# The last 32 tokens of a PEER layer leave the dense table products and are gathered instead

## The reference, cut to what matters

```
def peer(h, wq, subkeys, u_tab, v_tab):        # h: 256 x 1024; u_tab, v_tab: 16384 x 1024
    q = (h @ wq).reshape(256, 8, 2, 64)        # 8 heads, two halves
    s = einsum('thpd,hpnd->thpn', q, subkeys)  # 128 scores for each half
    sv, si = top_k(s, 16)
    cand = sv[:, :, 0, :, None] + sv[:, :, 1, None, :]      # 16 x 16
    best, pos = top_k(cand, 16)
    eidx = the expert numbers (row * 128 + column) of the 16 best
    gates = softmax(best)
    act = gelu(einsum('td,thkd->thk', h, u_tab[eidx]))
    w = gates * act
    return einsum('thk,thkd->td', w, v_tab[eidx])
```

## Time and profile before

| what | value |
|---|---|
| median of 3 runs | 1016.75 us |
| profiled execution, span of its instructions | 1014.6 us |
| what lies around the span (median less span) | about 2.15 us |
| PE busy | 998.4 us (98%) |
| DVE, ACT, POOL busy | 773.9, 506.5, 323.3 us |
| DMA | 222.78 MB, 220 GB/s over the span |

### The profile page before, as it was taken

One profiled execution on the slowest core, in us unless ns is written; L12 is line 12 of the kernel. 1 busy time (PEld: TensorE's weight loads), 2 busy tenths in 40 slices (PEclk: granted clock), 3 DMA queues, 4 the chain that ended last, 5 costly groups with the idle time before them and its releaser, 6 DMA issues.

```text
span 1014.6 us, 17813 instructions
## 1 busy us (share of the span) xinstructions
PE 998.4 (98%) x6803; PEld 920.8 (91%) x6803; DVE 773.9 (76%) x1580; ACT 506.5 (50%) x730; POOL 323.3 (32%) x206
## 2 busy tenths in 40 slices
PE   8999999999999999999999999999999999999996
PEld 8899889999999999999999999988888888888885
DVE  6979887883998798886678788766665867777666
ACT  4676556455444544445443443454554554454443
POOL 1001000112776678786778867000010000000002
PEclk9999999999999999999999999999999999999999
DMA  9989858776555687777666766677678788887761
GB/s 358 369 286 378 291 195 302 258 222 219 181 176 182 163 192 187 185 187 177 161 153 146 160 147 146 185 217 221 217 238 310 228 253 259 266 265 228 222 206 48
DMA packets 96852, 222.78 MB, mean 220 GB/s; under 512 B 27520, under 2 KB 45952, under 8 KB 96000
## 3 DMA queue, kind: packets, MB, share of 16 engines
q1 hardware_dynamic: 74336, 207.93, 63.4%
q0 software_dynamic: 22144, 13.71, 8.9%
q10 hardware_dynamic: 288, 0.01, 0.0%
HBM read 211.06 MB, written 10.55 MB: 218 GB/s over the span
## 4 chain that ended last, share of the span: by engine, by line
PE 88%; DVE 5%; DMA 2%; ACT 2%; issue 1%; POOL 1%; POOLq 0%; ACTq 0%; DVEq 0%
PE px L1148 33%; PE pw L842 16%; PE pw L843 16%; PE pw L844 16%; PE px L1124 3%; DMA raw<-in_w 2%; DVE w_lo L1204 1%; PE px L1093 1%; DVE lo L1226 1%; DVE ada L1243 0%; ACT hi L563 0%; PE px L1027 0%; ACT w_hi L563 0%; PE px L1010 0%; ACT h2f L734 0%
## 5 line engine op out<-in xcount | busy, mean ns | idle before, releaser
L563 ACT ACTIVATE w_hi<-raw 128x1024 fp32r<-128x1024 f32 x312 | 328.7, 1057 | 314.6 <-PE px L1148 151.7
L1204 DVE TENSOR_TENSOR w_lo<-raw,w_hi 128x1024 fp32r<-128x1024 f32 x285 | 347.3, 1225 | 134.1 <-ACT w_hi L563 131.7
L842 PE MATMUL pw<-a_hi,w_hi 128*128 128x256 f32 x1280 | 366.8, 287 | 0.3 <-DVE a_lo L1454 0.3
L844 PE MATMUL pw<-a_hi,w_lo 128*128 128x256 f32 x1280 | 362.1, 283 | 0.0
L843 PE MATMUL pw<-a_lo,w_hi 128*128 128x256 f32 x1280 | 362.1, 283 | 0.0
L536 POOL DMA_INDIRECT gates_spill<-gate,place x128 | 228.7, 1787 | 82.5 <-issue 47.2
L842 PEld LDWEIGHTS pw<-a_hi,w_hi 128*128 128x128 f32 x1280 | 245.4, 192 | 2.0 <-issue 1.2
L843 PEld LDWEIGHTS pw<-a_lo,w_hi 128*128 128x128 f32 x1280 | 245.5, 192 | 0.2
L844 PEld LDWEIGHTS pw<-a_hi,w_lo 128*128 128x128 f32 x1280 | 245.4, 192 | 0.0
L1148 PE MATMUL px<-w_hi,ws_hi 128*128 128x512 f32 x512 | 159.6, 390 | 0.2 <-DVE ws_lo L1653 0.2
L1148 PE MATMUL px<-w_lo,ws_hi 128*128 128x512 f32 x512 | 159.0, 389 | 0.0
(11 more groups left out here) (349 smaller groups left out, 1119.6 us busy)
## 6 DMA issues: line engine op xcount, KB each, us to landing
raw<-in_u SPq DMA_DIRECT2D x128, 512.0 KB, 4.4
raw<-in_v SPq DMA_DIRECT2D x128, 512.0 KB, 4.8
raw<-in_ws SPq DMA_DIRECT2D x56, 512.0 KB, 6.5
ada<-in_ada SPq DMA_DIRECT2D x20, 512.0 KB, 7.7
ada<-in_w_ada SPq DMA_DIRECT2D x16, 512.0 KB, 7.2
gates_spill<-zero POOLq DMA_DIRECT2D x16, 512.0 KB, 7.3
g_row<-gates_spill SPq DMA_DIRECT2D x128, 64.0 KB, 4.6
ada<-in_ada SPq DMA_DIRECT2D x6, 1024.0 KB, 10.4
```

The lines of the kernel that those rows point to most:

```text
L563: return nc.scalar.activation(out, in_, ACT.Copy, **kw)
L842: nc.tensor.matmul(out, lh, rh, start=start and x == 0, stop=False)
L844: last = nc.tensor.matmul(out, ll, rh, start=False, stop=stop and x == len(pairs) - 1)
L1204: v.tensor_tensor(w_lo[:, m % RING], raw[:, m % RING], w_hi[:, m % RING].bitcast(F32), ALU.subtract).then_inc(lo_ready, 1)
```

## The change

`NS` = 32 tokens (224 to 255) are taken out. `TD` = 224 tokens stay dense, `T1` = 96 of them in the second tile.

- U matmuls have 224 moving columns, not 256; `W`, `ws_hi`, `ws_lo` have 224 columns. There are 24 one-hot groups, not 32, every 13/8 pieces from piece 86 on (before: 11/8 from 82).
- V matmuls of the second tile have a stationary operand of 96 columns, with 512 moving columns as before.
- The 32 x 128 (token, expert) pairs are laid out as 128 partitions (4 groups of 32 tokens) x 32 numbers c. For each c POOL gathers 128 rows of the U table (4 KB each) with an indirect DMA to one of three buffers `sp_row`, multiplies them by the tokens' own input `h2_rep` (128 x 1024), and ACT sums each row (`accum_out`) after the row of `SUM_AT` (V rows 4 to 58). After Gelu (row 60) and the gates, POOL gathers the V rows one c at a time, and DVE adds gate x row to `sp_acc` after the row of `ADD_AT` (rows 64 to 118). Two matmuls with `sel` put the sum in the PSUM rows 96 to 127 before the last four rows.
- PE makes `h2_rep` by 16 matmuls (`repeated`) after group 40, with two ACT copies.
- The step `names` is made for 4 heads at a time (`places`, `matches`, `keyed`, `names`), and so are `gates`, Exp and `normal`. POOL splits 22 pieces, not 26; the scatter begins when the first 4 heads' gates are there.
- `g_row` comes 4 rows at a time; the order of the table in HBM is changed for it. The residual work moves from row 52 to row 88, `E_ROWS` from 36 to 42, `GT2_ROW` from 60 to 66. POOL issues its six loads after the last product.

```
+NS = 32
+TD = T - NS
+T1 = TD - P
+QUADS = P // NS
+POOL_PIECES = 22
+EXP_AFTER = (8, 16, 28, 38)
+NORMAL_AT = 79
+INDEX_AFTER = 40
+OH = T1 // 4
+OH_AT = [86 + 13 * n // 8 for n in range(OH)]
+SUM_AT = [4 + 7 * c // 4 for c in range(NS)]
+GELU_AT = SUM_AT[-1] + 2
+ADD_AT = [GELU_AT + 4 + 7 * c // 4 for c in range(NS)]
...
+GT2_ROW, GT2_LOAD, GT2_SUM, GT2_ADD = 66, 70, 72, 112
+G_ROWS = 4
...
@@ SP
+                if m == UP + 2 * INDEX_AFTER + 6:
+                    sp.wait_ge(sp_named, 1)
+                    sp.wait_ge(gate_ready, 2 * TT)
+                    for k in range(QUADS):
...
                 if m == VP:
                     sp.wait_ge(scattered, 16 * PH * TOPK)
-                    sp.wait_ge(oh_ready, OH)
-                    for r in range(RING):
-                        load_gates(r)
+                    sp.wait_ge(oh_used, OH)
+                    for n in range(2):
+                        load_gates(n)
...
@@ POOL
+            def fetch(table, x):
+                nc.gpsimd.indirect_dma_start(sp_row[x % 3][:, :], None, table, bass.IndirectOffsetOnAxis(
+                    ap=sp_idx[:, x % NS:x % NS + 1], axis=0)).then_inc(sp_row_landed[x % 3], 16)
...
+            pool.wait_ge(scattered, 16 * TOPK * PH)
+            pool.wait_ge(sp_landed, 32 * QUADS)
+            pool.wait_ge(idx_ready, 3)
+            for c in range(NS + 2):
+                if c < NS:
+                    if c >= 3:
+                        pool.wait_ge(sp_summed, c - 2)
+                    fetch(u_rows_d, c)
+                if c >= 2:
+                    fetched(c - 2)
+                    nc.gpsimd.tensor_tensor(sp_row[(c - 2) % 3][:, :], sp_row[(c - 2) % 3][:, :], h2_rep[:, :], ALU.mult) \
+                        .then_inc(sp_prod, 1)
             pool.wait_ge(piece_used, VP + E_ROWS)
...
+            pool.wait_ge(sp_summed, NS)
+            v_rows = v_d.rearrange("j i d -> (j i) d")
+            for c in range(NS):
+                if c >= 3:
+                    pool.wait_ge(sp_added, c - 1)
+                fetch(v_rows, NS + c)
...
@@ ACT, U stage
+                if g == INDEX_AFTER + 2:
+                    act.wait_ge(idxT_done, 2)
+                    for half in range(2):
+                        copy(h2_rep[:, half * 512:(half + 1) * 512], px[2 + half][:, :]).then_inc(idx_ready, 1)
...
@@ ACT, V stage
             for v in range(NK - RING):
                 split_hi(VP + v + RING)
                 split_w(v + RING)
+                if v in SUM_AT:
+                    c = SUM_AT.index(v)
+                    act.wait_ge(sp_prod, c + 1)
+                    copy(sp_row[c % 3][:, :], sp_row[c % 3][:, :], accum_out=sp_w[:, c:c + 1]).then_inc(sp_summed, 1)
+                if v == GELU_AT:
+                    act.wait_ge(sp_summed, NS)
+                    nc.scalar.activation(sp_w[:, :], sp_w[:, :], ACT.Gelu).then_inc(sp_summed, 1)
...
@@ PE
-                columns_piece(m, pw[g % 2][:, e * T:(e + 1) * T])
+                hi, lo = (w.rearrange("p (k c) -> p k c", k=KC) for w in weights(m))
+                three(pw[g % 2][:, e * TD:(e + 1) * TD], [(hi[:, k], lo[:, k], a_hi[:, k, 0:TD], a_lo[:, k, 0:TD])
+                                                          for k in range(KC)]).then_inc(piece_used, 1)
...
+            def repeated():
+                pe.wait_ge(gate_exp, 2 * TT)
+                pe.wait_ge(score_used, TT * PH)
+                for k in range(KC):
+                    out = px[2 + k // 4][:, (k % 4) * P:(k % 4 + 1) * P]
+                    for x, part in enumerate((rep_hi, rep_lo)):
+                        last = nc.tensor.matmul(out, part[:, k].rearrange("p q t -> p (q t)"), ident_r[:, :], start=x == 0, stop=x == 1)
...
+            for half in range(2):
+                nc.tensor.matmul(px[2 + half][T1:P, :], sel[:, :], sp_acc[:, half * 512:(half + 1) * 512], start=True, stop=True)
...
@@ DVE, V stage, after split_lo and split_w of row r
+                if r in ADD_AT:
+                    c = ADD_AT.index(r)
+                    x = NS + c
+                    row = sp_row[x % 3]
+                    if c == 0:
+                        dve.wait_ge(sp_summed, NS + 1)
+                        v.tensor_tensor(sp_w[:, :], sp_w[:, :], sp_gate[:, :], ALU.mult).then_inc(sp_added, 1)
+                    dve.wait_ge(sp_added, c + 1)
+                    dve.wait_ge(sp_row_landed[x % 3], 16 * (x // 3 + 1))
+                    if c == 0:
+                        ins = v.tensor_scalar(sp_acc[:, :], row[:, :], sp_w[:, 0:1], None, ALU.mult)
+                    else:
+                        ins = v.scalar_tensor_tensor(sp_acc[:, :], row[:, :], sp_w[:, c:c + 1], sp_acc[:, :], ALU.mult, ALU.add)
...
-                if r == E_ROWS + 16:
+                if r == 88:
```

More of the change, by code:

```diff
@@ L814, in _ @@
                     take_upper(OH_AT.index(2 * g + 1))
-                for t in range(TT):
-                    if g == EXP_AFTER[t]:
-                        act.wait_ge(best_ready, t + 1)
-                        nc.scalar.activation(gate[t][:, :], gate[t][:, :], ACT.Exp).then_inc(gate_exp, 1)
+                for n in range(2 * TT):
+                    if g == EXP_AFTER[n]:
+                        h = slice(n % 2 * 4, n % 2 * 4 + 4)
+                        act.wait_ge(best_ready, n + 1)
+                        if n == 3:
+                            copy(ident_r[:, :], ident[:, :])
+                            for wide, part in ((rep_hi, a_hi), (rep_lo, a_lo)):
+                                copy(wide[:, :, :, :], part[:, :, TD:T].unsqueeze(2).broadcast_to([P, KC, QUADS, NS]))
+                        nc.scalar.activation(gate[n // 2][:, h], gate[n // 2][:, h], ACT.Exp).then_inc(gate_exp, 1)
             for v in range(NK - RING):
@@ L1571, in _, with names @@
+            def names(t, n):
+                need(at["key"])
+                at["last"] = go(v.tensor_reduce(ij[t][:, :, 4 * n:4 * n + 4].rearrange("p a h k -> p h a k"),
+                                                eq[:, :, :, :].rearrange("p (h a) k c -> p h a k c", a=2), AX, ALU.add))
             at = {}
-            steps = (upper_half, lower_half, candidates, best_eight, next_eight, names)
-            def gates(t):
+            steps = (upper_half, lower_half, candidates, best_eight, next_eight)
@@ L1625, in _ @@
+            for i in range(PH - 1):
                 for step in steps:
                     step(i)
-            gates(0)
-            upper_half(PH)
-            lower_half(PH)
+                if i == 3:
+                    places()
+                    matches()
+                    keyed()
+                    names(0, 0)
+                    gates(0, 0)
+                if i == 5:
+                    normal(0, 0)
             dve.wait_ge(lo_ready, lo_count(UP + POOL_PIECES - 1))
             m = UP + POOL_PIECES
-            for i in range(PH, TT * PH):
-                for n, step in enumerate(steps):
+            for i in range(PH - 1, TT * PH):
+                for step in steps:
@@ L1634, in _ @@
                     split_lo(m)
                     m += 1
[L1636 to L1640 removed]
+                    step(i)
+                if i == PH:
+                    normal(0, 1)
+                if i % 4 == 3:
+                    t, n = i // PH, i // 4 % 2
+                    split_lo(m)
+                    places()
+                    matches()
+                    split_lo(m + 1)
+                    keyed()
+                    split_lo(m + 2)
+                    m += 3
+                    names(t, n)
+                    gates(t, n)
```

194 lines of the change are left out of this document (110 added, 84 removed).

## The result

The changed kernel takes 1038.28 us (median of 4 runs, 1036.90 to 1041.19); the kernel before, on the same chip, 1016.56 us (4 runs). The ratio is 1.0216, 95% interval 1.0200 to 1.0232: 22 us slower. I had predicted 1029 us, 12 slower. The profiled execution has a span of 1037.1 us against 1014.6.

The account below looks back on a forecast made before the run. PE, 98% busy, bounds the kernel, besides any engine that comes late. U stage 29.9 us less and V stage 41.8 more give +12, so 1029 us; likeliest 1020 to 1040 (35%), range 1000 to 1055.

Parts of the forecast that it names:

- U pairs, -24.6: U stage: 3072 load and matmul pairs go from 0.120 to 0.112 us apart, 24.6 us gained (0 to 41).
- The load as floor: U stage: loading 128 stationary columns limits a load and matmul pair to 0.112 us, above the columns' 0.1067.
- One-hots and `repeated`, -5.3: U stage: eight fewer one-hot groups save 7.1 us, `repeated` adds 1.8; its waits cost 0, at most 3.
- U sums, +28: V rows 4 to 58: gather, product and sum take 5.86 us per number, so PE loses 28 us (5 to 60).
- rival A: V's U sums: cheap gathers and little port wait keep the cycle to 4.77 us; 1003 us in total, 25%.
- The lock's price: V's U sums: POOL's product and DVE's row work exclude each other; POOL waits 0.3 us (0 to 1.2).
- Rival C: V's U sums: no lock between POOL and DVE, cycle 5.56 us; +3, 1020 us in total, 10%.
- Start of the additions, +8: V near row 64: the first V gather lands behind POOL's six loads, DVE waits; PE loses 8 us (0 to 12).
- Row 88, +3: V row 88: four residual DVE instructions meet a gt2 and a V addition; 3 us lost (0 to 5).
- DMA +1: V around row 88: DMA should carry 374 GB/s against the 349 seen; 1 us lost (0 to 5).
- `sel`, +1.8: V stage on PE: two float32 `sel` matmuls, 4 records of 0.43 us each, add 1.8 us.
- The second tile's 96 columns: V stage on PE: 512 columns still move and the load stays hidden, so the narrower operand costs 0.

Follow-up runs that it names:

- e4: Changed kernel with U matmuls of 192 moving columns, not 224, so the last 32 aren't made: 1038.99 us, one run.
- e6: Changed kernel with POOL's six loads issued one at a time between V gathers: 1038.13 us.
- e1: Changed kernel without the sparse part (no gathers, products, sums, additions or `sel` matmuls; last 32 tokens get no value): 997.33 us, ratio 0.9813.
- e10: e5 without the V half of the sparse part (no V gathers, additions or `sel`): 998.68 us, one run.
- e12: e9 with all V products 128 tokens wide and ring columns 224 to 255 filled once: 992.91 us, one run.
- e9: e1 with `ws_hi` and `ws_lo` rows of 256 numbers at their old place and `g_row` moved: 993.12 us, one run.
- e8: e1 with the second tile's stationary operand 128 columns wide again, not 96: 998.32 us, one run.
- e5: Changed kernel with each U product and sum as one DVE instruction; POOL only gathers, ACT's sums gone: 1008.9 us, ratio 0.9919.

## Why the prediction was right in its direction, and 10 us short

The mechanism held: U gains, the U sums and the additions cost V more. It is luck in part that the forecast missed by no more: what U gained less than forecast, 2.6 us, and what the V terms were too high, 2.6, cancel. Term by term, predicted and measured:

- *U pairs, -24.6.* 111.7 ns apart against 119.9: 3072 x 8.2 = -25.2. The load as floor was right, and e4 shows it. The Trainium skill's 107 ns for a load of 128 columns ("TensorE: Matmul & The Clock Gate", LDWEIGHTS) is 5 ns under what e4 and the changed kernel measured for a load with its matmul; the measurement decides.
- *One-hots and `repeated`, -5.3, with 0 for its waits.* `repeated` ran as predicted, 480.88 to 482.69 with no stall. But V started 27.3 us earlier, not 29.9. The stall at 352 was not foreseen (two matmul starts 2.6 us apart): DVE waits 6.0 us for ACT's Exp of 4 heads' gates. The prediction took `names` for 4 heads as hidden and gave the gates no term. PE also waits 0.8 us longer than before at V's first matmul.

```profile
352.69 0.22 DVE L1700 TENSOR_REDUCE gsum<-gate 128x4 f32<-128x64 f32 x1 [6.00 <-ACT gate L889]
```

- *U sums, +28.* The lateness at row 60 is 25.9 less 3.0 of drift: 22.9, of which some 1.7 is the clock. The cycle is 5.57 us, not 5.86: on POOL a U gather takes 0.98 or 1.88 us (mean 1.40), below the 1.86 taken from the earlier trace rows. By the prediction's own words it is wrong if the gather takes under 1 us; half of them do, and the cycle still stayed above the 4.77 of the plan. So rival A was half right. The lock's price lies on the other side than I had it: I gave POOL a wait of 0.3 us, and its product is 2.48 us long for 2.40, but 78 us of DVE were stopped. PE's gaps are not the 0.5 us in each row that were forecast, but 1.8 us every 22.5 us. The Trainium skill ("SBUF — State Buffer", Who interferes with whom) calls the port pair that the two share an exclusive lock; the 3.21 us where 0.28 is usual agree. Rival C, no lock, falls by the same rows. The row of before from which the lock was read, 2.46 us long, is a TENSOR_SCALAR with one tile and a column as inputs, not a product of two SBUF tiles; it was weaker evidence than the prediction makes of it, and the rows above carry the claim.
- *Start of the additions, +8.* Rows 60 to 68: 36.3 - 25.9 - 0.4 = 10.0. From row 64 on it is 7.1, from the wait that was named; about 3 of it is the clock at its lower level, which the prediction hadn't. The other 2.9 are the waits for the gates' rows and the piece behind the six loads, which it hadn't either. As a price it held; as a saving it did not (e6).
- *Row 88, +3, and DMA +1.* 2.7 and, up to row 120, 1.9.
- *`sel`, +1.8.* From row 120 to 127 lateness grows by 2.4 us, and by 0.7 in e1 and e10, which have no `sel`: 1.7.
- *The second tile's 96 columns, "0".* This is the term that failed: V's matmuls stand 231.1 ns apart, not 226.7, and the stage without sparse work (e1) is 6.3 us longer than before. The prediction reasoned that 512 columns still move and the load is hidden; e12 shows that the operand's width and its ring's rows set the time all the same.
- *The tail, no term.* POOL's DRAIN, +5.2, moves the end by 4.3. No row of before could show it: with its 128 scatters the DRAIN took 2.82 us.

The misses add up: drift 6.3, DRAIN 4.3, V's start 2.6, and the V terms -2.6 (28 + 8 + 3 + 1 + 1.8 = 41.8 predicted, 22.9 + 10.0 + 2.7 + 1.9 + 1.7 = 39.2 measured): 10.6, what lies between +11.9 and +22.5.

## What to carry to other kernels

Put elementwise work on the idle engine only after asking what it locks: here the same 32 products and sums cost 23 us less on the fuller VectorE, in one instruction each, than on POOL and ACT beside it. Ask of a burst of loads which other transfers it delays, not only the one behind it in its queue. Count a chain that alternates engines (gather, product, sum) by its sum, not by each engine's room. And when an operand's shape changes, its matmuls' pace is a term with bounds, even where the column count stays; so is what an engine must still close after its last instruction.

## What the runs showed of the hardware

- V matmuls of 512 columns stand 226.7 ns apart (rows without a stall) with 128-wide operands from ring rows of 256 numbers, 230.0 with 96-wide ones from the same rows, 231.4 with 128-wide ones from rows of 224, and 231.1 with both changed (e12, e9, e8, e1).
- POOL's DRAIN at the end grows by 0.082 us for each gather of 128 rows of 4 KB (2.82, 5.44, 8.05 us with 0, 32, 64); with the 128 scatters and no gather it is 2.82.
- The granted clock fell to the 1.2 GHz level behind some PE stalls (two matmul starts 2.35 to 10.7 us apart) and not behind others of 2.6 to 3.1 us: after the stall at 352 it fell in eight of the thirteen profiles that have it and not in five. At half for 3.4 us it costs up to 1.7 us, for 6.8 us up to 3.4.
- DVE's row instructions of 0.28 to 1.22 us become up to 5.5 us long beside POOL's products of 128 x 1024. With the same 32 gathers and no product (e5) none is lengthened.
- A gather's time on POOL isn't one number: mostly 0.98 or 1.88 us in the U sums (mean 1.40; 1.83 in e5), 0.94 to 5.02 us in the V additions, where the DMA moves 328 GB/s (855 to 1000 us).
